# Block-diagonal gates of the recurrent half: four 64x64 products on the quadrants of TensorE in place of two 128x128 products with zero blocks

## What is computed

```python
xb = x.reshape(B_, S, A_BLOCKS, A_BLOCK)
r = sigmoid(einsum('bsnc,ncd->bsnd', xb, w_a).reshape(B_, S, A_WIDTH) + b_a)
i = sigmoid(einsum('bsnc,ncd->bsnd', xb, w_x).reshape(B_, S, A_WIDTH) + b_x)
log_a = RG_C * r * log_sigmoid(lam)
a = exp(log_a)
u = sqrt(-expm1(2.0 * log_a)) * (i * x)
h = associative_scan(a, u)
```

## Time and profile before

| | |
|---|---|
| Median of 3 runs | 1589.89 us |
| The three runs | 1588.66, 1589.89, 1593.15 us |
| Span of the profiled execution | 1591.2 us, 26973 instructions |
| TensorE matmul busy | 1540.1 us, 97% |
| VectorE, ScalarE, GpSimd busy | 35%, 22%, 13% |
| Mean granted TensorE clock | 0.995 of full speed |

### The profile page before, as it was taken

One profiled execution on the slowest core, in us unless ns is written; L12 is line 12 of the kernel. 1 busy time (PEld: TensorE's weight loads), 2 busy tenths in 40 slices (PEclk: granted clock), 3 DMA queues, 4 the chain that ended last, 5 costly groups with the idle time before them and its releaser, 6 DMA issues.

```text
span 1591.2 us, 26973 instructions
## 1 busy us (share of the span) xinstructions
PE 1540.1 (97%) x11592; PEld 793.3 (50%) x11592; DVE 553.2 (35%) x1277; ACT 346.0 (22%) x577; POOL 211.1 (13%) x256
## 2 busy tenths in 40 slices
PE   7999999999999999898999999999999999999987
PEld 4444555544444444443566666646544444444442
DVE  4222635322222222225244444445322222222225
ACT  3131621010000000003444555432010000000003
POOL 5000000000000000000244444420010000000000
PEclk9999999999999999999999999999999999999999
DMA  8621056999999999997421112115999999999996
GB/s 301 248 75 53 27 224 260 401 413 427 427 426 426 427 427 426 427 420 308 182 84 54 54 60 94 61 45 233 359 408 428 427 426 426 427 426 427 426 421 257
DMA packets 59403, 472.22 MB, mean 297 GB/s; under 512 B 12929, under 2 KB 12937, under 8 KB 31376
## 3 DMA queue, kind: packets, MB, share of 16 engines
q1 hardware_dynamic: 54336, 462.51, 70.5%
q0 software_dynamic: 4800, 7.87, 1.3%
q10 hardware_dynamic: 144, 0.05, 0.0%
HBM read 452.03 MB, written 24.27 MB: 299 GB/s over the span
## 4 chain that ended last, share of the span: by engine, by line
PE 49%; DMA 3%; DVE 1%; issue 1%; ACT 1%; POOLq 0%; SPq 0%; DVEq 0%; ACTq 0%
PE ps L828 13%; PE ps L663 11%; PE ps L1069 11%; PE ps L843 6%; PE ps L628 3%; DMA sb_ring<-in_w_up_dram 2%; PE ps L1087 2%; DMA sb_ring<-expert_rows 1%; PE ps L834 1%; PE ps L993 0%; PE ps L1128 0%; DVE sb_h L2033 0%; PE ps L1004 0%; ACT sb_work L1203 0%; PE ps L1096 0%
## 5 line engine op out<-in xcount | busy, mean ns | idle before, releaser
L828 PE MATMUL ps<-sb_ring,sb_work 128*56 128x512 f32 x2048 | 453.2, 595 | 18.3 <-issue 15.2
L828 PEld LDWEIGHTS ps<-sb_ring,sb_work 128*56 128x56 f32 x2048 | 147.6, 130 | 310.6 <-issue 310.3
L843 PE MATMUL ps<-sb_ring,sb_work 128*56 128x512 f32 x1024 | 230.9, 593 | 0.6 <-DMA sb_ring<-in_w_down_dram 0.6
L663 PE MATMUL ps<-sb_work,sb_h 128*64 128x112 f32 x4096 | 223.8, 263 | 0.0
L663 PEld LDWEIGHTS ps<-sb_work,sb_h 128*64 128x64 f32 x4096 | 206.1, 139 | 34.3 <-issue 30.8
L1491 POOL DMA_INDIRECT expert_rows<-sb_work,sb_ri x60 | 54.9, 915 | 1118.3 <-DVE sb_work L1883 720.5
L1874 DVE TENSOR_TENSOR sb_work<-sb_work,ps 56x512 f32<-56x512 f32 x64 | 70.0, 1093 | 322.3 <-ACT sb_work L1306 322.2
L1069 PE MATMUL ps<-sb_work,sb_ring 128*128 128x512 f32 x384 | 172.3, 603 | 2.0 <-ACT sb_work L1203 2.0
L1306 ACT ACTIVATE sb_work<-ps 56x512 f32<-56x512 f32 x64 | 37.7, 589 | 437.4 <-PE ps L828 437.4
L843 PEld LDWEIGHTS ps<-sb_ring,sb_work 128*56 128x56 f32 x1024 | 67.2, 130 | 113.4 <-issue 112.3
L1321 ACT ACTIVATE sb_work<-ps 56x512 f32<-56x512 f32 x60 | 35.5, 591 | 393.1 <-PE ps L843 355.4
(11 more groups left out here) (240 smaller groups left out, 1214.3 us busy)
## 6 DMA issues: line engine op xcount, KB each, us to landing
sb_ring<-in_w_down_dram SPq DMA_DIRECT2D x62, 2048.0 KB, 25.4
sb_ring<-in_w_gate_dram SPq DMA_DIRECT2D x54, 2048.0 KB, 21.9
sb_ring<-in_w_up_dram SPq DMA_DIRECT2D x54, 2048.0 KB, 26.4
sb_ring<-in_w_gate_dram SPq DMA_DIRECT2D x18, 1024.0 KB, 25.4
sb_ring<-in_w_up_dram SPq DMA_DIRECT2D x18, 1024.0 KB, 27.8
sb_ring<-in_c_w_in_dram SPq DMA_DIRECT2D x8, 2048.0 KB, 12.0
sb_ring<-in_ab_w_in_dram SPq DMA_DIRECT2D x5, 2048.0 KB, 15.1
expert_rows<-sb_work SPq DMA_DIRECT2D x2, 4096.0 KB, 20.4
```

The source lines that it names most:

```text
L663: mm = nc.tensor.matmul(dst[64 * z:64 * z + 64], a[:, 64 * z:64 * z + 64], b, start=start, stop=stop)
L828: mm = nc.tensor.matmul(dst[64 * z:64 * z + CAP, :], me["xgT"][:, j, c, q * CAP:(q + 1) * CAP], wblock(slots[z], NC)[:, c, :], start=(c == ...
L843: mm = nc.tensor.matmul(dst[64 * z:64 * z + CAP, :], src[:, c * CAP:(c + 1) * CAP], wblock(slots[2], FC)[:, c, z * 512:(z + 1) * 512], sta ...
```

## The change

The job pair (`ra`, `ix`) of a group m becomes (`even`, `odd`), in the same banks. For each m TensorE first waits for both banks, then makes four products of 64 rows by 64 columns by 512 tokens, in this order: wa of the even block to the low half of bank `even`; wa of the odd block to the high half of bank `odd`; wx of the even block to the high half of bank `even`; wx of the odd block to the low half of bank `odd`. Even blocks read partitions 0 to 63, odd blocks 64 to 127, so each bank receives from one row half only. `fills` comes with each bank's second product. ScalarE empties each bank in two Sigmoids of 64 partitions by 512, 16 in all in place of 8. The `r` half stays on its partitions, the `i` half is moved to the other 64. Its bias is read from a new tile `bx_turned`, `b_x` with its halves exchanged, which VectorE makes with two copies of 64x4 between lines 1707 and 1709. The zeroing of `wa` and `wx` and the DMAs are as before.

```diff
+        bx_turned = sb("bx_turned", [P, 4])
...
+        bias_turned = sem("bias_turned")
...
         for m in range(4):
-            bk.add(("ra", m), 4 + m % 2)
-            bk.add(("ix", m), 6 + m % 2)
+            bk.add(("even", m), 4 + m % 2)
+            bk.add(("odd", m), 6 + m % 2)
...
             for m in range(4):
                 pe.wait_ge(xc_ready, m + 1)
-                for name, w in (("ra", m0["wa"]), ("ix", m0["wx"])):
-                    dst = opens((name, m))
-                    fills(nc.tensor.matmul(dst[:], w[:, m, :], m0["xc"][:, m, :], start=True, stop=True), (name, m))
+                even, odd = opens(("even", m)), opens(("odd", m))
+                low_rows, high_rows = slice(0, 64), slice(64, P)
+                for w, cols_even, cols_odd in ((m0["wa"], low_rows, high_rows), (m0["wx"], high_rows, low_rows)):
+                    for dst, rows, part in ((even, low_rows, cols_even), (odd, high_rows, cols_odd)):
+                        mm = nc.tensor.matmul(dst[part], w[rows, m, rows], m0["xc"][rows, m, :], start=True, stop=True)
+                        if w is m0["wx"]:
+                            fills(mm, ("even" if rows is low_rows else "odd", m))
...
             for m in range(4):
-                for name, dst, b in (("ra", "r", "b_a"), ("ix", "i", "b_x")):
-                    wait_full(act, (name, m))
-                    drains(A(m0[dst][:, m, :], bank((name, m))[:], ACT.Sigmoid, bias=at[b][:, m:m + 1]), (name, m))
+                for job, r_rows, i_from, i_to in (("even", slice(0, 64), slice(64, P), slice(0, 64)),
+                                                  ("odd", slice(64, P), slice(0, 64), slice(64, P))):
+                    wait_full(act, (job, m))
+                    A(m0["r"][r_rows, m, :], bank((job, m))[r_rows, :], ACT.Sigmoid, bias=at["b_a"][r_rows, m:m + 1])
+                    if m == 0:
+                        act.wait_ge(bias_turned, 2)
+                    drains(A(m0["i"][i_to, m, :], bank((job, m))[i_from, :], ACT.Sigmoid, bias=bx_turned[i_from, m:m + 1]),
+                           (job, m))
...
             for m in range(4):
-                wait_drained(act, ("ra", m))
+                wait_drained(act, ("even", m))
+                wait_drained(act, ("odd", m))
...
+            v.tensor_copy(bx_turned[64:P, :], at["b_x"][0:64, :]).then_inc(bias_turned, 1)
+            v.tensor_copy(bx_turned[0:64, :], at["b_x"][64:P, :]).then_inc(bias_turned, 1)
             lam, u, w, acc = at["lam"], lamt[:, 1, :], lamt[:, 2, :], lamt[:, 3, :]
...
             for m in range(4):
-                wait_drained(dve, ("ix", m))
-                wait_drained(dve, ("ra", m))
+                wait_drained(dve, ("even", m))
+                wait_drained(dve, ("odd", m))
             v.tensor_tensor(m0["i"], m0["i"], m0["xc"], ALU.mult).then_inc(rg_x, 1)
```

## The result

The changed kernel takes 1594.27 us (median of 7 runs, 1593.73 to 1598.14) against 1589.36 us (median of 7, 1587.92 to 1593.15) before: ratio 1.0028, 95% interval 1.0016 to 1.0039. It is slower, by an amount of the size that I had called indistinguishable: the ratio lies just inside 0.3%, and the median is 0.27 us above the top of my range, 1594.0. A loss is shown, since the interval excludes 1. In the medians it is 4.9 us, by the ratio 4.5. The forecast of 1590.1 was 4 us too low, and its likeliest case is not what happened.

A forecast was written before the change was run, and what follows sets the result against it. TensorE was taken to bound the kernel; its 3.4 us saved in the gates goes into two waits for ScalarE, k starts 0.2 us later and all else is covered, so 1589.89 + 0.2 gives 1590.1 us. Range 1587.8 to 1594.0.

The forecast's parts named there:

- likeliest case: Whole kernel: four quadrants at once, TensorE's saving lost in waits for ScalarE, 0.2 us later, 1590.1 us; chance 0.49.
- What bounds the kernel: Whole kernel: TensorE, busy 1540.1 of 1591.2 us, so its delays nearly always become kernel time; it sets the gate stage.
- TensorE's part: Gate products: 6.87 us removed; four quadrants at once take 0.86 us a group, 3.44 us for all.
- two at once: Gate products: only two quadrants run together, +1.7 us, 1591.6 us; chance 0.2.
- None at once: Gate products: quadrants queue, stage 13.8 us, +6.9 us, 1596.8 us; chance 0.04.
- ScalarE's part: Gate Sigmoids: half the rows cost the full 687 ns; 16 take 9.6 us (11.0 at most), where it was 6.7.
- the 0.594 us between neighbours: Gate Sigmoids: back to back they overlap by 0.093 us, so they start 0.594 us apart.
- my upper end 0.687: Gate Sigmoids: 0.687 us apart if changing partitions prevents overlap; k starts 0.8 us later.
- The clock: TensorE in the gates: works only 3.4 of 7 us, so its clock may fall, 1.74 us lost; not in the forecast.
- Behind it: After the gates: ScalarE ends 2.9 us later, but evictions, VectorE's chain and ya_ready have cover; copies hidden, tile shift 0.
- the clock rival: TensorE from the gates on: granted clock falls, 1592.1 us, up to 1593.9 if it comes twice; chance 0.24.
- Half the rows at half the price: Gate Sigmoids: 16 take today's time, TensorE freed, up to -3.4 us, 1586.5 us; chance 0.03.

The follow-up runs named there:

- e3_eight_banks: Changed kernel with a bank of its own for each of the eight gate jobs, k in banks 4 to 7, v in 0 to 3: 1587.98 us, ratio 0.9976.
- e1_tile_last: Changed kernel with the new tile bx_turned allocated behind all other tiles, so every other tile lies as before: 1594.58 us, ratio 1.0022.
- e2_fill: Changed kernel with TensorE kept busy in its two stalls, two unneeded full products before group 2 and one before group 3: 1592.0 us, ratio 1.0012.
- e6_halves_paired: Kernel before with 16 straight Sigmoids of 64x512, ordered so every second neighbour stays on its partition half: 1593.84 us, one run.
- e7_full_twice: Kernel before with each gate's 128x512 Sigmoid made twice, the first into tiles free then: 1594.53 us, one run.

## Why the prediction was right or wrong

*What bounds the kernel*: right. What the start of `k` gains or loses comes back in the time: -3.28 us in the stage of e3_eight_banks gave 3.8 less by the ratio (interval 2.2 to 5.6) and 3.2 in the medians, the changed kernel's 3.05 us in the stage and `k` gave 4.5 more (2.5 to 6.2), and the 4.21 of e1_tile_last 3.5 more (1.6 to 5.4).

*TensorE's part*: right, with the sum near exact. All four quadrants run at once; 32 records take 3.59 us up to `k` where I had 3.44 and 0.15 for the change of shape. The rival "two at once", and with it the strict reading of the Trainium skill (TensorE: Matmul & The Clock Gate, Part 3) that weight loads wait where the row group is in use, falls: four loads of 129 ns lie together, two of them on each row half. "None at once" falls too.

*ScalarE's part*: right that rows are free (0.68 us for 64 rows) and that TensorE's gain turns into two waits. Wrong in one term: **the 0.594 us between neighbours**. It was taken from four activations that all used 128 partitions. The measured 0.70 is even above my upper end 0.687. Seven distances stand before group 3's banks are free, so this is 7 x 0.106 = 0.74 us of the path. My sum put `k` 104.36 - 97.4 = 6.96 us behind the first product, and e2_fill, without the clock, has 7.90. The other 0.2 us are a later first Sigmoid (1.14 us behind the first product, not 1.05) and 0.15 us, not 0.05, from the end of the eighth Sigmoid to group 3 (103.62 to 103.77). The wait of 2.1 us before group 2 was 1.7 in the forecast, for the same reason.

*The clock*: the step that failed. I gave its fall 0.24 and left it out of the forecast, and priced it at 1.74 us from the earlier trace rows. It fell in the changed kernel and in its variant with the tile moved, and by the mean clocks in most of their runs; against e2_fill it cost 1.9 us in one profile and 3.1 in the other. I took as comfort a stretch in which 2.92 of 4.50 us busy had kept the clock; but its one long wait is 1.51 us, while here one is 2.1 us; and in e6_halves_paired the clock fell behind that very wait of 1.51 us (0.57 from 208 to 212). The row to go by was the other one: the fall at 747 came behind a wait of 2.04 us. Such a wait does not settle it either: the same place of after, above, has 2.02 us and the clock held, and the kernel before kept it through 2.40 us at 643.77. What decides it in the single case stays open. With the right distance between the Sigmoids and the fall as the likeliest case the sum would have been +0.2 + 0.7 + 1.74, about 1592.5, which is still 1.8 us under the median.

*Behind it*: right. `ya_ready`, `k`'s and `v`'s evictions, the copies of `bx_turned` and the shift of the tiles cost nothing that a run shows.

*The rivals*: the clock rival won, together with the upper end of the Sigmoids' spacing, to which I had not joined it. Its sums have a slip: 1590.1 + 1.74 is 1591.8, not 1592.1, and with 1.74 twice 1593.6, not 1593.9. That the upper one is within 0.7 us of the result is luck: it stands for two falls, and each profile has one behind the gates. The same luck put the top of my range next to the result. "Half the rows at half the price" falls. What stays open is the rest: 3.05 us in stage and `k` against 4.5 by the ratio and 4.9 in the medians. The interval holds both, and the same stretch lost 4.21 us in e1_tile_last, so executions differ in it by more than a microsecond; no run points to a second place.

## What to carry to other kernels

When TensorE gets faster on a stage that feeds PSUM, count the evictions and the banks before the products: an eviction of 64 partitions costs as much as one of 128, so cutting them in half doubles the other engine's work, and then a plan of two banks per result hands the whole gain back as a wait. A wait of TensorE can cost more than itself: here 1.0 us for the waits, and 1.9 us in one profile and 3.1 in another for the clock that fell behind them. Giving each result a bank of its own, which here took three lines, turned the same change from a loss of 0.28% into a gain of 0.24%.

## What the runs showed that I had not expected

- Neighbouring activations of 512 elements out of PSUM start 0.57 to 0.59 us apart on the same partitions and 0.70 us apart when the half that is read or written changes. In e7_full_twice the starts stay 0.57 us apart while the time shown for one grows from 0.69 to 0.79 us: the distance of the starts is the price, not the duration.
- Eight records of 64x64 products with 512 columns (four products) take 1.09 us at full clock and 1.98 us at half; at full clock each further group adds 0.86 us (32 records in 3.66).
- After 2.1 us without a product the granted clock was 0.50 for about 6.7 us in one execution, and in another it held through the same wait (group 2 in 1.09 us) and fell within the second one, of 1.72 us. Products of no use, put into the waits, kept it at 1.00 and saved 0.9 us up to `k` and 1.9 up to `v`.
- At other places of this kernel the clock falls in some executions and not in others, for 1.7 us mostly; near 1548 in e1_tile_last the work took 13.46 us in place of 10.51. Spans of single executions differ by that much without any change.
